# Second block's attention with keys and values per head, and two heads in one array, in place of the absorbed latent

## The reference, cut to what matters

```python
c = rms_norm(c_kv, kv_g)                                   # (S, 128), shared by the heads
qh = q.reshape(bsz, seq, ATT_HEADS, ATT_HEAD_DIM)          # 8 heads of 64
q_lat = einsum('bshd,hcd->bshc', qh, w_uk) * (ATT_HEAD_DIM ** -0.5)
# per block of 128 queries: sel = top_k(index_score, 256), c_sel = c[sel]
s = einsum('bthc,btkc->bthk', ql_b, c_sel)
s = where(valid, s, neg)
p = softmax(s, axis=-1)
o_lat = einsum('bthk,btkc->bthc', p, c_sel)
out = einsum('bshc,hcd->bshd', o_lat, w_uv)
# after it: mixed = concat(att * silu(gate_a), ssm * silu(gate_s)); y = mixed @ w_out;
#           layer_norm(ALPHA * x + y)
```

## Time and profile before

| | us |
|---|---|
| median of 3 runs (2855.95 to 2858.24) | 2856.73 |
| the profiled execution: span from first to last instruction | 2849.9 |
| TensorE busy, whole span | 2699.3 (95%) |
| TensorE busy, 2550 to 2813 us | 252.49 of 263.00 |
| VectorE busy, same stretch | 158.35 |
| ScalarE busy, same stretch | 90.97 |
| attention stage with its preparation | 2517.8 to 2849.9 |

### The profile page before, as it was taken

One profiled execution on the slowest core, in us unless ns is written; L12 is line 12 of the kernel. 1 busy time (PEld: TensorE's weight loads), 2 busy tenths in 40 slices (PEclk: granted clock), 3 DMA queues, 4 the chain that ended last, 5 costly groups with the idle time before them and its releaser, 6 DMA issues.

```text
span 2849.9 us, 32261 instructions
## 1 busy us (share of the span) xinstructions
PE 2699.3 (95%) x12315; PEld 1935.7 (68%) x12315; DVE 1315.3 (46%) x2098; ACT 843.5 (30%) x1499; POOL 347.4 (12%) x463
## 2 busy tenths in 40 slices
PE   6999999799999989999998999999989999989997
PEld 4856999686666868569997866668556655444553
DVE  3253555321111332535553211113578999955763
ACT  3232444421111322324444211113152212133332
POOL 0012221000000000022210000000043554200000
PEclk9998999899999999989999999999999999999999
DMA  5010000011111230100000111112400011010000
GB/s 185 26 60 1 1 1 1 30 28 46 46 46 44 89 123 26 60 1 1 1 1 30 26 46 46 46 45 89 127 30 9 30 38 37 30 60 30 30 15 30
DMA packets 104843, 114.81 MB, mean 40 GB/s; under 512 B 20304, under 2 KB 76208, under 8 KB 104688
## 3 DMA queue, kind: packets, MB, share of 16 engines
q1 hardware_dynamic: 104688, 112.69, 12.5%
HBM read 94.73 MB, written 16.78 MB: 39 GB/s over the span
## 4 chain that ended last, share of the span: by engine, by line
PE 88%; DVE 4%; ACT 3%; issue 2%; DMA 1%; POOL 1%; SPq 1%; DVEq 0%; ACTq 0%; POOLq 0%
PE PS L643 8%; PE PS L572 7%; PE PS L613 6%; PE PS L619 6%; PE PS L616 6%; PE PS L551 6%; PE PS L735 5%; PE PS L441 4%; PE PS L964 4%; PE PS L561 4%; PE PS L657 2%; PE PS L660 2%; PE PS L663 2%; PE PS L877 2%; PE PS L832 2%
## 5 line engine op out<-in xcount | busy, mean ns | idle before, releaser
L613 PE MATMUL PS<-hHi,R2aR 128*128 128x512 f32 x768 | 306.4, 399 | 14.9 <-DVE R2aR L1708 14.9
L616 PE MATMUL PS<-hLo,R2aR 128*128 128x512 f32 x768 | 300.4, 391 | 0.0
L619 PE MATMUL PS<-hHi,R2aR 128*128 128x512 f32 x768 | 300.3, 391 | 0.0
L572 PEld LDWEIGHTS PS<-R,R2b 128*128 128x128 f32 x2048 | 250.2, 193 | 26.4 <-issue 12.6
L572 PE MATMUL PS<-R,R2b 128*128 128x64 f32 x2048 | 245.9, 274 | 12.2 <-ACT R2b L1264 12.2
L1259 ACT ACTIVATE R2b<-PS,negm 128x1024 f32<-128x1024 f32 x128 | 142.8, 1115 | 259.9 <-DVE negm L1686 259.9
L1708 DVE TENSOR_TENSOR R2aR<-W,R2aR 128x1024 fp32r<-128x1024 f32 x48 | 57.4, 1223 | 318.2 <-ACT R2aR L1292 318.2
L1686 DVE TENSOR_REDUCE negm<-PS 128x1 f32<-128x1024 f32 x128 | 156.7, 1224 | 75.9 <-PE PS L551 74.9
L1312 ACT ACTIVATE R3a<-PS,pT 128x512 f32<-128x512 f32 x64 | 42.3, 688 | 467.3 <-PE PS L619 467.3
L613 PEld LDWEIGHTS PS<-hHi,R2aR 128*128 128x128 f32 x768 | 145.3, 189 | 48.4 <-issue 18.7
L616 PEld LDWEIGHTS PS<-hLo,R2aR 128*128 128x128 f32 x768 | 145.2, 189 | 33.2 <-issue 3.3
(11 more groups left out here) (345 smaller groups left out, 4844.9 us busy)
## 6 DMA issues: line engine op xcount, KB each, us to landing
W<-in_w_in SPq DMA_DIRECT2D x10, 2048.0 KB, 8.5
W<-in_w_in SPq DMA_DIRECT2D x33, 512.0 KB, 4.8
xres<-R SPq DMA_DIRECT2D x3, 4096.0 KB, 19.2
W<-in_w_out SPq DMA_DIRECT2D x6, 2048.0 KB, 7.8
R<-xres SPq DMA_DIRECT2D x2, 4096.0 KB, 17.6
W<-in_c_dft_s SPq DMA_DIRECT2D x2, 2052.0 KB, 8.8
R<-in_x SPq DMA_DIRECT2D x1, 4096.0 KB, 12.9
W<-in_w_in SPq DMA_DIRECT2D x4, 1024.0 KB, 7.4
```

What stands on the lines that cost most here:

```text
L572: mm = pe.matmul(PS[:, 6, t * VD:(t + 1) * VD], PT[u % 2][:, k * P:(k + 1) * P], v_tok[:, k, h, :], start=(k == 0), stop=(k == 7))
L613: mm = pe.matmul(o, wHi[c % 2][:, k, :], hHi[:, k, ns], start=(k == 0), stop=False)
L616: mm = pe.matmul(o, wHi[c % 2][:, k, :], hLo[:, k, ns], start=False, stop=False)
L619: mm = pe.matmul(o, wLo[c % 2][:, k, :], hHi[:, k, ns], start=False, stop=(k == 7))
```

## The change

TensorE now computes keys per head pair (`kT2`, 8 products of 512 columns) and values for all heads (`v2`, 8 products) before the loop, instead of the absorbed queries. Keys lie with an even head in partitions 0 to 63 and the odd one in 64 to 127. The loop on TensorE goes by pairs p of heads: `scores2(p)` computes both heads, each in its half of the array's rows, into banks 0, 1 and 2, 3. `pv_pair2` multiplies values (64 columns of weights) by the transposed probabilities, one head in each half of the array's columns, and leaves the output transposed already, so that `latent_out`, `att_out` and `att_turn` go. The division by the softmax's sums now has to be done along the free dimension: the inverted sums go to DRAM and come back spread over partitions, by four transfers per tile. The output projection runs half a tile to a tile later. On VectorE and ScalarE the loop still goes head by head. The diff, cut:

```diff
-LATE = [(3, 7)] + [(t, h) for t in (4, 5, 6) for h in (1, 3, 5, 6, 7)]
+LATE = [(3, 7)] + [(t, h) for t in (4, 5, 6) for h in (1, 2, 5, 6, 7)]
...
             for m in range(4):
                 for n in range(2):
-                    b = (1 + 2 * h + n) % 8
+                    b = 2 * m + n
                     o = begin(b)
-                    pe.matmul(o, wukT[r_, h // 2, :], qT2[r_, h // 2, n * 512:(n + 1) * 512],
+                    pe.matmul(o, wuk[:, m * P:(m + 1) * P], c2T[:, n * 512:(n + 1) * 512],
                               start=True, stop=True).then_inc(full[b], 1)
+            for t in range(NT):
+                o = begin(t)
+                pe.matmul(o, c2T[:, t * P:(t + 1) * P], wuv, start=True, stop=True).then_inc(full[t], 1)
...
-            def scores2(u):
...
+            def scores2(p):
+                t, m = p // 4, p % 4
+                begin(0)
+                begin(2)
                 w = (t + 1) * P
                 for n in range((w + 511) // 512):
+                    for e in range(2):
+                        r_ = slice(VD * e, VD * e + VD)
+                        mm = pe.matmul(PS[:, 2 * e + n, 0:min(512, w - 512 * n)], qT2[r_, m, t * P:(t + 1) * P],
+                                       kT2[r_, m, n * 512:min(w, n * 512 + 512)], start=True, stop=True)
+                        if n == (w - 1) // 512:
+                            mm.then_inc(full[2 * e], 1)
...
+            def pv_pair2(p):
+                t, m = p // 4, p % 4
+                pe.wait_ge(free[4], pt2[2 * p + 1][0])
+                pe.wait_ge(free[5], pt2[2 * p + 1][1])
+                if m == 0:
+                    begin(6)
                 for k in range(t + 1):
+                    for e in range(2):
+                        h = 2 * m + e
+                        mm = pe.matmul(PS[VD * e:VD * e + VD, 6, m * P:(m + 1) * P], v2[:, k, h * VD:(h + 1) * VD],
+                                       PT2[(2 * p + e) % 4][:, k * P:(k + 1) * P], start=(k == 0), stop=(k == t))
...
+            for p in range(4 * NT):
+                t, m = p // 4, p % 4
+                if p + 1 < 4 * NT:
+                    scores2(p + 1)
+                p_turn2(2 * p)
+                if p >= 1:
+                    pv_pair2(p - 1)
+                if m < 2 and t >= 2:
+                    out_half(t - 2, 0, m)
+                if m >= 2 and t >= 1:
+                    out_half(t - 1, 1, m - 2)
+                p_turn2(2 * p + 1)
+            pv_pair2(4 * NT - 1)
+            for half in range(2):
+                out_half(NT - 2, 0, half)
+            for half in range(2):
+                out_half(NT - 1, 1, half, 4)
+            for half in range(2):
+                out_half(NT - 1, 0, half, 5)
...
             for t in range(NT):
+                sp.wait_ge(s2_ri, t + 1)
+                for e in range(2):
+                    sp.dma_start(rsums2[t, e].rearrange("m q -> q m"), rinv[:, H * t + e:H * t + H:2],
+                                 allow_slow_non_contiguous=True).then_inc(s2_rw, 16)
+                sp.wait_ge(s2_rw, 32 * (t + 1))
+                for e in range(2):
+                    small(rbc[t % 2][VD * e:VD * e + VD].rearrange("p m c -> p (m c)"),
+                          rsums2[t, e].rearrange("m q -> (m q)").partition_broadcast(VD), s2_bc)
...
-                if t >= 2 and h == 2:
+                if t >= 2 and h == 6:
                     ln_std(t - 2)
...
+            def sums_inverted(t):
+                dve.wait_ge(free[2], sums2[t])
+                dve.reciprocal(rinv[:, H * t:H * t + H], rsum[:, H * t:H * t + H]).then_inc(s2_ri, 1)
 
             def att_gate(t):
                 o = arrive(6)
+                dve.wait_ge(s2_bc, 32 * (t + 1))
+                dve.tensor_tensor(att, o.rearrange("p (m c) -> p m c", m=4), rbc[t % 2], ALU.mult).then_inc(free[6], 1)
+                dve.wait_ge(free[6], bk.count(6))
                 m = mix[:, 0:4, t * P:(t + 1) * P]
+                dve.tensor_tensor(m, m, att, ALU.mult).then_inc(s2_gate, 1)
...
                 if t >= 2:
                     if h == 0:
-                        residual(t - 2, 0)
+                        residual(t - 2, 1)
                     if h == 4:
+                        residual(t - 2, 0)
+                    if h == 7:
                         layer_norm(t - 2)
                 if t >= 1:
                     if h == 1:
+                        sums_inverted(t - 1)
                     if h == 3:
                         att_gate(t - 1)
-                    if h == 6:
-                        residual(t - 1, 1)
```

More of the change, by code:

```diff
@@ L927, in p_turn2, with out_half @@
                 pt2[u] = (bk.count(4), bk.count(5))
[L929 to L955 removed]
+            def pv_pair2(p):
[4 more added lines that the diff above has]
+                    begin(6)
+                for k in range(t + 1):
+                    for e in range(2):
+                        h = 2 * m + e
+                        mm = pe.matmul(PS[VD * e:VD * e + VD, 6, m * P:(m + 1) * P], v2[:, k, h * VD:(h + 1) * VD],
+                                       PT2[(2 * p + e) % 4][:, k * P:(k + 1) * P], start=(k == 0), stop=(k == t))
+                if m == 3:
+                    mm.then_inc(full[6], 1)
+            def out_half(t, n, half, b=7):
                 if (n, half) == (1, 0):
[L958 removed]
+                    pe.wait_ge(s2_gate, t + 1)
                     if t == 0:
@@ L1131, in _ @@
                       a["w_out_2"][0, :, n * 512:(n + 1) * 512].rearrange("(k p) c -> p k c", p=P))])
-            sp.wait_ge(full[0], marks["qlat"])
+            for b in range(8):
+                sp.wait_ge(full[b], marks["attention"][b])
             small(lng, a["ln_g_2"][0].partition_broadcast(P), s2_ln)
@@ L1135, in _ @@
             sp.wait_ge(s_xsave, 16 * (L + 1))
+            for t in range(2):
+                small(xt[t], xres[t * P:(t + 1) * P, :], s2_xt[t])
             for t in range(NT):
-                if t >= 2:
-                    sp.wait_ge(s2_od[t % 2], 16 * (t // 2))
-                small(xt[t % 2], xres[t * P:(t + 1) * P, :], s2_xt[t % 2])
+                sp.wait_ge(s2_ri, t + 1)
[6 more added lines that the diff above has]
+                          rsums2[t, e].rearrange("m q -> (m q)").partition_broadcast(VD), s2_bc)
                 if t >= 1:
@@ L1473, in ln_std, with turned_high @@
                                ).then_inc(s2_sq, 1)
+            bk.n = list(marks["attention"])
+            def turned_high(u):
+                t = u // H
+                if t < 4:
+                    return
+                o = arrive(5)
+                w = (t - 3) * P
+                act.activation(PT2[u % 4][:, 512:512 + w], o[:, 0:w], ACT.Copy).then_inc(free[5], 1)
             for u in range(H * NT):
                 t, h = u // H, u % H
-                if u >= 1:
-                    tp = (u - 1) // H
-                    hp = (u - 1) % H
-                    bk.take(4)
-                    if tp >= 4:
-                        o = arrive(5)
-                        n = tp - 3
-                        act.activation(PT2[hp // 4][:, 4:4 + n, (hp % 4) * P:(hp % 4 + 1) * P],
-                                       o[:, 0:n * P].rearrange("p (k c) -> p k c", k=n), ACT.Copy).then_inc(free[5], 1)
                 b = 2 * (u % 2)
-                bk.take(b)
                 act.wait_ge(s2_nm, u + 1)
@@ L2056, in turned @@
             def turned(u):
-                t, h = u // H, u % H
-                n = min(4, t + 1)
+                t = u // H
+                w = min(4, t + 1) * P
                 o = arrive(4)
```

180 lines of the change are left out of this document (50 added, 130 removed).

## The result

| | before | after |
|---|---|---|
| median | 2856.55 us | 2999.93 us (2993.89 to 3000.77) |
| profiled span | 2849.9 | 2999.0 |
| attention stage with preparation | 2517.8 to 2849.9: 332.1 | 2523.5 to 2999.0: 475.5 |

The ratio of after to before is 1.0498, interval 1.0483 to 1.0512. 143.4 us of the 149.1 between the spans lie in the changed stage.

The account below looks back on a forecast made before the run. TensorE was taken to bound the loop before. Its remaining work, new waits and extra work sum to 390 us against 332, +58; lost clock adds 42: span 2950, median 2956 us, 100 slower; range 2898 to 2998.

Parts of the forecast that it names:

- TensorE's work at full clock, with switches: TensorE's products in preparation, loop and tail, plus array mode switches: 13.7 + 185 + 13 + 22.5, 234 us.
- waits before the scores: TensorE idle before a pair's scores: 72 for the return, 63 of extra work less 12; with 5.9 of preparation, 129 us.
- waits for the sums and VectorE's steps behind them: TensorE's values and tail wait for the sums' DRAM way and VectorE: 12 us in the loop, 4.4 in the tail.
- half clock: TensorE's granted clock drops behind long idle stretches: 18 x 2.35 = 42 us, bounds 0 and 81.
- the new wait: Between pairs, TensorE's next scores wait for copy, mask and exponential in a row: 72 us over 31 returns.
- the work and the halves: TensorE's loop and tail work falls by 76 us, less 5 preparation and 13 switches, with array halves running side by side.
- rival (2): Array halves don't overlap in the loop: scores cost 29 us more, values 35; near 2995 us, chance 0.08.
- each leg taken as the 2.6 us of an output write: The sums' DRAM way, two writes and two reads: 6 us with issue; tile 1 waits 4.2.
- 18 idle stretches reach 4.2 us: TensorE's idle stretches in tiles 1 to 7 and the tail that cost clock, 2.35 us each, 42 in all.
- the extra work: VectorE and ScalarE steps falling in the return (rounds, residuals, layer norm, sums' way): 63 us, selection rounds 15.3 of it.
- The 6.8: The runs' median stood 6.8 us above the profiled span; added to the 2950 us span for the 2956 forecast.
- Rival (3): The return is covered because head 2p+3's mask need not wait for transposes of 2p+1: -58, 2799 us, chance 0.05.

Follow-up runs that it names:

- e6: Changed kernel without the sums' DRAM way and division, both heads' transposes before the projection quarter, scores waiting for masks instead of exponentials; 2879.92 us.
- e7: e6 with four buffers for the probabilities in place of two, and transposes copied two heads late instead of one; 2856.71 us.
- e9: e7 with one line moved: VectorE adds a residual at head 5 instead of head 4; 2832.35 us.
- e10: e8 with the residual at head 5, spread sums in bank 5 copied by ScalarE, projection quarter behind both transposes in a tile's first pair; 2818.21 us.
- e11: e10 with the values' products ordered one head after the other, not in alternating column halves; 2826.16 us.
- e1: Changed kernel without the sums' four DRAM transfers per tile, the softmax's division left out; 2962.01 us.
- e4: Changed kernel with the 16 late selection rounds all at odd heads instead of six at heads 2 and 6; 3000.39 us.
- e3: Changed kernel with 328 unused filler products on TensorE where it otherwise waits; 2970.26 us.
- e8: e7 with the division restored, sums spread by TensorE without DRAM, selection rounds over tiles 1 to 6, some steps reordered; 2857.93 us.

## Why the prediction was right in kind and too small

The forecast was 2956, the range ended at 2998, the result is 2999.9. Its parts against the trace of after, in us (measured: TensorE's busy time in the stage is 306.7, its idle time the other 168.8):

| term | predicted | measured |
|---|---|---|
| TensorE's work at full clock, with switches (13.7 + 185 + 13 + 22.5 of the tail) | 234 | 306.7 - 68.4 = 238.3 |
| waits before the scores (72 + 63, less the 12 below) and 5.9 for the layer norm's vectors | 129 | 115.0 |
| waits for the sums and VectorE's steps behind them (12 in the loop, 4.4 in the tail) | 16 | 32.5 + 8.1 = 40.6 |
| half clock | 42 | 68.4 |
| end behind the last product | 11 | 11.4 |
| others | 0 | 1.7 |
| stage | 432 | 475.4 |

**Right: the new wait.** The scores of a pair wait for the exponential that closes the pair before, 114.0 us over 31 returns, where 100 to 130 was given. The experiments took its links away: the exponential behind the mask (e6), the shared buffer and the early copy, both at once (e7), the residual in the way (e9). With all gone the wait is 2.5 us (e10), though part of it only moved: 15.3 us stand before the transposes, where after had 0.9.

**Right: the work and the halves.** TensorE's work in the stage at full clock fell from 299.5 - 3.3 = 296.2 to 238.3 us, by 57.9; the prediction's sum for it was 76 - 5 - 13 = 58. Preparation took 2543.08 - 2523.53 = 19.6, as forecast. In e10 a pair of tile 7 takes 2760.03 - 2750.73 = 9.30 us from scores to scores. The prediction's paces give 1.7 + 16 x 0.109 + 32 x 0.060 + 3.43 + 0.4 of switches = 9.2; rival (2), no overlap, is out, and e11 shows what it would look like for the values.

The Trainium skill ("TensorEngine Tiling (Array Packing)", Key Properties) states that a change of the tiling mode drains the array. The trace agrees as far as it goes: without the 0.4 the sum is 8.8, and 9.30 was measured. No run takes the switches out alone, so that the 0.5 between them is theirs isn't shown.

**Wrong: "each leg taken as the 2.6 us of an output write", 6 us for the sums' way.** It is 15 us, of which the write of single floats takes 8.8. The row it was taken from the earlier trace rows is a transfer of long runs; no row read before showed one of single floats, and the step was given no upper bound. It made the waits of this term 24 us longer than forecast. e1 splits the term: with the DRAM way gone 7.9 and 4.4 us are left, against 7.8 and 4.4 forecast for VectorE's steps; the way itself, forecast to make TensorE wait 4.2 us in tile 1 alone, cost the 28.3.

**Wrong: "18 idle stretches reach 4.2 us", with only these costing clock.** 20 stretches reached 4.2 us, near the count, but the trace has 28 stretches at half clock: some followed shorter idle times. In tile 7 the scores behind 2.85 us of idle time also took 3.52 us:

```profile
2914.43 3.52 PE L914 MATMUL PS<-R,R3a 64*128 64x512 f32 x8 [2.85 <-ACT R3b L1485]
```

The rows named only what had dropped the clock (5.4 and 4.75 us of idle), not what would not. The mean price of one came out near the forecast, 68.4/28 = 2.4 against 2.35, but that is in part luck: the first of the 28, 41 us long, cost 9.5 us, the last nothing. The term is 26 us too small. Its upper bound of 81 did hold it. The last slices of PEclk read 0.6 to 0.8, below the 0.8 to 0.9 forecast.

**Wrong in size: the extra work.** The term of 63 us priced rounds at even heads at 15.3; e4 moved them all, 7 us of the scores' wait went and the total stayed. The total of the scores' waits was forecast 14 us too high, which by luck covered part of the two misses. (Two small misreadings go with it: the copy is 0.69 us in rows 4 and not 0.61, and the last product ends at 2839.5 by rows 3 and not at 2839.2.)

The two wrong sizes, 24 and 26, less 14 of the waits and with 4 of work and 2 of the rest, are the 43 us between 432 and 475. The span stands 5.7 more above the 2950 forecast for it, by the scatter ahead of the stage, and the median came out 0.9 above the span and not 6.8, which together make the 44 us between 2956 and 2999.9. The 6.8 had been taken for time around the span; that, too, fell out by luck against the 5.7.

Rival (3), faster, named a condition that was needed and not enough: that the mask of head 2p+3 need not wait for the transposes of 2p+1. e7 meets it and is as long as before; only with the residual moved (e9) did it come out faster, and e10 adds the whole computation. e10's stage of 294.3 stands 20 above the rival's 332 - 58 = 274, of which the spreading of the sums (10.1 + 2.3 us busy) and the clock (12.7 against 3.3 before) are the whole; with them paid the change gains 38 us on the stage of before.

## What to carry to other kernels

When a change makes an engine's work coarser (two heads per step where there was one), write down from its last product to its next the row of steps on the other engines, and see whether each could have been started earlier; here a change that takes 58 us of work off TensorE lost 143 and, with the chain cut, won 38. Release a buffer by its last reader, and never put a wait for that engine's newest result ahead of a step that it needs next (one line, 24 us). Price a transfer from a row whose runs are as short as its own, and give it an upper bound where there is none; price the clock by every idle stretch that a trace does not show to be harmless.

## What the runs showed of the hardware

- A write of 2 KB from 128 partitions in single floats took 8.8 us to land in the median, a tile of 512 KB 2.7 (after).
- Adding 80.8 us of useless products made the kernel 30 us faster through the granted clock (e3); in e10 it stayed at 1.00 from 2620 to 2780 us, with TensorE idle for 6% of the time and for 1.3 us at most at once.
- Records of 128 columns with 64 columns of weights cost 0.060 us in alternating column halves and 0.10 one half after the other (e11). Eight records of 512 columns in alternating row halves cost 1.92 us from start to start with the switch, 0.24 each (e10), against 0.429 at full height.
- A reciprocal on 8 x 128 numbers took 0.95 us, longer than a copy of 128 x 512 (0.69), both from PSUM (e8).
